# A context feed-forward network in plain fp32, and expert gates made on GpSimd, in a two-block transformer kernel

## The chip, the cores and the metric

One program runs on one core of a Trainium2 chip. The metric is the device time of one execution in microseconds. The engines are TensorE (PE in the rows; its weight loads are PEld), VectorE (DVE), ScalarE (ACT), GpSimd (POOL) and SyncE (SP), which issues most of the DMAs; each works through its own instruction list in order and waits on semaphores.

## The reference, cut to what matters

Two transformer blocks run one after the other, the second with two layers. The first block ends in an expert layer (`peer_ffn`): each of 512 tokens takes 8 heads x 16 experts out of 128 x 128 experts, and their gates weigh the experts' outputs. Layer 0 of the second block also carries a context stream of 256 tokens through mixers and a network of its own; layer 1 needs only the mixers' input of it.

```
    cv, ci = lax.top_k(cand.reshape(t, PEER_HEADS, PEER_TOPK * PEER_TOPK), PEER_TOPK)
    ...
    gates = jax.nn.softmax(cv, axis=-1).reshape(t, PEER_HEADS * PEER_TOPK)
...
def swiglu(h, w_gate, w_up, w_down):
    return (jax.nn.silu(h @ w_gate) * (h @ w_up)) @ w_down
...
        if need_ctx_out:
            xc = xc + g1c * yc
            hc = rms_norm(xc, norm_ffn[i]) * (1.0 + sc2c) + sh2c
            xc = xc + g2c * swiglu(hc, w_gate[i], w_up[i], w_down[i])
```

D_MODEL is 1024, D_FF 2816, and all arithmetic is float32.

## The kernel before, in words

**Slabs and units.** The weights come as slabs of 128 x 1024 floats (512 KB) into four landing slots `raw0` to `raw3`, issued by SP in the order of a list called `spine`. One slab is one unit of matmul work: eight 128 x 128 blocks. A normal unit is computed in three matmuls of type fp32r for each block: the slab is split into an upper part `whi` (ScalarE, L517) and a lower part `wlo` (VectorE or GpSimd, L525), the activations are split too (`hchi`/`hclo`, or `f10h` pairs inside the network), and the program adds whi x hi (L559), whi x lo (L561) and wlo x hi (L570): 24 fp32r matmuls a unit. The first two units after a norm are interleaved (`pair_tensor`, L589, L591, L596). A landing slot may be loaded again when its lower part has been made. A few small products stay plain fp32: one such matmul stands in the trace as two rows, an fp32r one as one row.

**The context network.** `cnet`, of class `Network`, has 66 units with 256 token columns: 44 for gate and up and 22 for down, in two halves of 11 hidden tiles. For each hidden tile ScalarE makes the silu (L3084 makes the upper half of the product), VectorE the product (L3072) and its lower half (L3076). The network's input comes from a norm applied in `Apply` (`c0ffn`: plain value `hct_plain`, then an upper and a lower part). Behind the network stand the norm of layer 1's context mixer (`c1mix`: sums L653 and L656) and that mixer's units and chains (called the c1 stage below); its last results are copied to `c_res` and stored by SP (L2369). Then come the 384-column units of the expert layer.

**Dense groups.** The gates of 384 tokens are spread into a dense 128 x 128 table per token. Work goes in 96 groups of four tokens. For a group k, VectorE compares an iota with the two halves of the expert number of every slot (L3403, one instruction for the two one-hots of four tokens, ring of four buffers `onehot`), ScalarE (48 groups, L3414, four instructions) or GpSimd (48, L3431) multiplies one of them by the gates, TensorE makes four plain fp32 128 x 128 matmuls (L3388, eight rows), ScalarE copies them to `stage` (L3422), and SP stores every fourth group in one DMA of 1 MB to `gate_dram`. A route stream must have finished a tile of 128 tokens before its 32 groups may begin. `gin0` and `gin1` are blocks of that table loaded back for the expert layer. The first expert rows are fetched by GpSimd with indirect DMAs (L3591) and dotted on VectorE (L3549).

**The order.** A planner written in Python (`Weave`) runs once when the program is built. It keeps a clock for each engine with costs from `Blank`, opens the units in spine order, puts a piece of the side streams (routing, dense groups, mixers' chains) between the ticks of a unit when its clocks say that the piece is ready, and writes each engine's instructions in a fixed order. On the chip only that order and the semaphores count. `split_ahead` puts splits up to two units ahead; `pump` releases side pieces. Where something must be complete (`drain`), what is left of the side streams is put in one block.

Of the kernel before, what the change touches and what calls it, by code (L numbers as in the profile page):

```python
# [367 lines left out]
class Unit:  # L368


    def __init__(self, kind, key, slab, n, groups, ring, lo="vector"):
        self.kind, self.key, self.slab, self.n, self.groups, self.ring, self.lo = kind, key, slab, n, groups, ring, lo
        self.each, self.need = False, None
# [49 lines left out]
def program(nc, io):  # L423
# [111 lines left out]
    def split_gpsimd(g, i):  # L535
        if spine[i].lo == "gpsimd":
            split_lower(g, i)

# [130 lines left out]
    class Apply:  # L669
# [3 lines left out]
        def __init__(self, name, nm, use, pairs, gain, shift=None, late=(), once=False, before=None, eps=EPS, tap=None,  # L673
                     root=True):
            self.name, self.nm, self.use, self.gain, self.shift, self.late = name, nm, use, gain, shift, late
            self.once, self.before, self.eps, self.tap, self.root = once, before, eps, tap, root
            self.pairs = [Pair(p.hi, p.lo, ("apply_a", name, "hi", c), self.lower_sig(c), p.plain) for c, p in enumerate(pairs)]
# [4 lines left out]
        def scalar(self, a):  # L682
# [31 lines left out]
        def vector(self, v):  # L714
# [11 lines left out]
            for c in range(3, KC) if self.once else [KC - 1]:  # L726
                self.lower_vector(v, c)

        def gpsimd(self, g):
            if self.once:  # L730
                for c in range(3):
# [2291 lines left out]
    class Network:  # L3023


        def __init__(self, l, v, n, pairs, places, ring, lo, free):
            self.l, self.v, self.n, self.free, nm = l, v, n, free, f"f{v}{l}"
            self.name = nm
            self.hid = [[sb(f"{nm}h{k}{y}", places[2 * k + y], [n], F32R)[:] for y in range(2)] for k in range(HALF)]
            self.sg = [sb(f"{nm}sg{i}", places[2 * HALF + i], [n])[:] for i in range(2)]  # L3030
            self.units = []
            for half in range(2):
                for k in range(HALF * half, HALF * half + HALF):
                    for kind, w in (("fgate", "w_gate2"), ("fup", "w_up2")):
                        u = Unit(kind, (self, k), io[w][l * 22 + k], n, [Group(pairs, (self, k))], ring, lo[half])
                        u.frees = (lambda out: [("ffn_a", out[0].name, "gate", out[1])]) if kind == "fgate" else \
                            (lambda out: [("ffn_v", out[0].name, "lo" if out[0].v else "up", out[1])])
                        self.units.append(u)
                for s in range(HALF):
                    groups = []  # L3040
                    for b in range(8 * s, 8 * s + 8):
# [3 lines left out]
                        groups[-1].pairs.append(Pair(*self.hid[k], ("ffn_a", nm, "hi", HALF * half + k), ("ffn_v", nm, "lo", HALF * half + k)))  # L3045
                        groups[-1].closes = k == HALF - 1
                    u = Unit("fdown", (self, half, s), io["w_down2"][(l * 2 + half) * HALF + s], n, groups, ring, lo[half])
                    u.frees = lambda out: [(x_flag(out[0].v), "down" if out[1] else "halfdown", out[0].l, out[2])]
                    self.units.append(u)

    def fgate_scalar(a, i, phase):
        f, k = spine[i].key
        a.wait_ge(*end(i))
        if k >= 2:
            a.wait_ge("ffn_v", f.name, "lo", k - 2)
# [6 lines left out]
    def product(f, k):  # L3062

        return held(("out", "fup", (f, k)))[:, 0:f.n] if f.v else f.sg[k % 2]
# [13 lines left out]
    def fup_scalar(a, i, phase):  # L3078
        f, k = spine[i].key
        if phase:  # L3080
# [1196 lines left out]
```

## Time and profile before

| | us |
|---|---|
| three runs, median | 3979.23 |
| lowest and highest | 3978.86 to 3980.32 |
| span of the profiled execution | 3975.2 |
| PE busy in it | 3796.6 (96%) |
| DVE busy | 2398.2 (60%) |
| ACT busy | 1638.3 (41%) |
| POOL busy | 775.2 (20%) |

The span is the time from the first to the last recorded instruction of one profiled execution; it is 4.0 us under the median of the runs, and what lies around it (the start and end of an execution) is in the runs' time and not in the span. Busy time of TensorE counts overlapping matmul records once.

### The profile page before, as it was taken

How to read it: one execution, taken by the hardware profiler on the slowest of the kernel's cores; microseconds unless marked ns; L12 is line 12 of the kernel's file. 1: busy time of each engine (PE TensorE's matmuls, PEld its weight loads, DVE VectorE, ACT ScalarE, POOL GpSimd, SP SyncE). 2: the span in 40 equal slices, each digit the busy share in tenths (PEclk: the TensorE clock that was granted, in tenths of full speed). 3: DMA queues.
4: the chain of work that ended last, by engine and by line, in shares of the span. 5: the costliest groups of instructions: out<-in, count | busy, mean ns of one | idle time of the engine just before them, and what ended most of it. 6: DMA issues, size and time to landing. Idle time of an engine off the chain costs nothing.

```text
span 3975.2 us, 57159 instructions
## 1 busy us (share of the span) xinstructions
PE 3796.6 (96%) x23057; PEld 3298.6 (83%) x23057; DVE 2398.2 (60%) x4113; ACT 1638.3 (41%) x2622; POOL 775.2 (20%) x622
## 2 busy tenths in 40 slices
PE   8999999989998889999999999998899999889998
PEld 5788776778898789999999999786678877667887
DVE  6455333546899977777777776557633345664333
ACT  4523342444456653333333333536522233563222
POOL 0112000244137443332223331201100010101000
PEclk9999999999999999999999999998999999999999
DMA  5211235533355488888888886311233342202332
GB/s 200 83 46 44 102 118 204 174 98 99 123 190 179 165 297 285 286 281 289 270 288 277 283 284 188 113 58 60 82 120 134 122 143 69 74 27 86 99 97 75
DMA packets 209190, 617.28 MB, mean 155 GB/s; under 512 B 18464, under 2 KB 68640, under 8 KB 205088
## 3 DMA queue, kind: packets, MB, share of 16 engines
q1 hardware_dynamic: 168352, 465.76, 35.8%
q0 software_dynamic: 40576, 147.87, 10.8%
q8 instruction: 183, 3.00, 0.3%
q14 instruction: 79, 0.65, 0.1%
HBM read 583.67 MB, written 29.88 MB: 154 GB/s over the span
## 4 chain that ended last, share of the span: by engine, by line
PE 81%; DVE 9%; ACT 5%; DMA 3%; issue 2%; POOL 0%; SPq 0%; DVEq 0%; ACTq 0%; POOLq 0%
PE ps L559 23%; PE ps L570 22%; PE ps L561 22%; PE ps L2468 1%; DVE hlo_plain L719 1%; PE ps L2495 1%; PE ps L842 1%; DMA raw<-w_in 1%; ACT whi L517 1%; DVE onehot L3403 1%; PE ps L2076 1%; PE ps L2486 1%; DMA gate_dram<-stage 1%; PE ps L1173 1%; PE ps L1164 1%
## 5 line engine op out<-in xcount | busy, mean ns | idle before, releaser
L525 DVE TENSOR_TENSOR wlo<-raw,whi 128x1024 fp32r<-128x1024 f32 x576 | 711.6, 1236 | 646.1 <-ACT whi L517 645.5
L559 PE MATMUL ps<-hhi,whi 128*128 128x512 f32 (+1 forms) x2824 | 1078.8, 382 | 18.2 <-ACT uact L3475 9.8
L561 PE MATMUL ps<-hlo,whi 128*128 128x512 f32 (+1 forms) x2824 | 1051.5, 372 | 0.1
L517 ACT ACTIVATE whi<-raw 128x1024 fp32r<-128x1024 f32 x660 | 695.2, 1055 | 629.8 <-PE ps L570 489.1
L570 PE MATMUL ps<-hhi,wlo 128*128 128x512 f32 (+1 forms) x2824 | 669.3, 375 | 0.0
L559 PEld LDWEIGHTS ps<-hhi,whi 128*128 128x128 f32 x2824 | 534.6, 189 | 120.7 <-issue 25.9
L561 PEld LDWEIGHTS ps<-hlo,whi 128*128 128x128 f32 x2824 | 535.0, 189 | 68.9 <-issue 4.1
L570 PEld LDWEIGHTS ps<-hhi,wlo 128*128 128x128 f32 x2824 | 512.6, 189 | 74.2 <-issue 7.2
L559 PE MATMUL ps<-ag_hi,whi 128*128 128x384 f32 x1024 | 342.7, 335 | 0.0
L561 PE MATMUL ps<-ag_lo,whi 128*128 128x384 f32 x1024 | 342.2, 334 | 0.0
L525 POOL TENSOR_TENSOR wlo<-raw,whi 128x1024 fp32r<-128x1024 f32 x85 | 206.6, 2441 | 162.3 <-ACT whi L517 162.2
L3591 POOL DMA_INDIRECT fetched<-peer_v_rows,rows x128 | 152.0, 1187 | 360.6 <-DVE xtok L3563 337.5
L3591 POOL DMA_INDIRECT fetched<-peer_u_rows,rows x128 | 151.5, 1183 | 340.9 <-DVE ract L3549 335.4
L3475 ACT ACTIVATE uact<-ps 128x384 f32<-128x384 f32 x128 | 62.9, 491 | 363.8 <-PE ps L570 363.8
L570 PE MATMUL ps<-ag_hi,wlo 128*128 128x384 f32 x1024 | 198.2, 334 | 0.0
L561 PEld LDWEIGHTS ps<-ag_lo,whi 128*128 128x128 f32 x1024 | 192.4, 188 | 0.0
L559 PEld LDWEIGHTS ps<-ag_hi,whi 128*128 128x128 f32 x1024 | 192.3, 188 | 0.0
L559 PE MATMUL ps<-hchi,whi 128*128 128x256 f32 x672 | 171.1, 290 | 16.2 <-ACT c_res L1935 4.6
L570 PEld LDWEIGHTS ps<-ag_hi,wlo 128*128 128x128 f32 x1024 | 179.3, 188 | 0.0
L3492 DVE TENSOR_TENSOR uact<-uact,gin 128x384 f32<-128x384 f32 x128 | 71.4, 558 | 163.6 <-ACT uact L3475 152.3
L644 POOL COPY nacc<-nsq 128x512 f32<-128x512 f32 x6 | 3.7, 609 | 851.2 <-ACT nsq L633 851.2
L561 PE MATMUL ps<-hclo,whi 128*128 128x256 f32 x672 | 167.2, 285 | 0.0
(653 smaller groups left out, 6233.1 us busy)
## 6 DMA issues: line engine op xcount, KB each, us to landing
raw<-w_in SPq DMA_DIRECT2D x151, 512.0 KB, 3.6
raw<-peer_u SPq DMA_DIRECT2D x128, 512.0 KB, 4.6
raw<-peer_v SPq DMA_DIRECT2D x128, 512.0 KB, 4.2
raw<-w_mod SPq DMA_DIRECT2D x96, 512.0 KB, 3.9
raw<-w_gate SPq DMA_DIRECT2D x66, 512.0 KB, 3.5
raw<-w_up SPq DMA_DIRECT2D x66, 512.0 KB, 3.5
raw<-w_down SPq DMA_DIRECT2D x66, 512.0 KB, 3.5
gate_dram<-stage SPq DMA_DIRECT2D x24, 1024.0 KB, 4.8
```

The costliest lines, as they stand in the source:

```text
L517: a.x.activation(whi[n % NW][:], raw[i % NRAW][:], ACT.Copy, bias=0.0, scale=1.0).then_inc(*a.gives("hi", i))
L525: e.x.tensor_tensor(wlo[n % NW][:], raw[i % NRAW][:], whi[n % NW][:].bitcast(F32), ALU.subtract).then_inc(*e.gives(*lo_sig(i)))
L559: t.x.matmul(o, w, p.hi, start=grp.opens and k == 0, stop=False)
L561: t.x.matmul(o, w, p.lo, start=False, stop=False)
L570: ins = t.x.matmul(o, lo[:, 128 * (starts[gi] + k):128 * (starts[gi] + k) + 128], p.hi, start=False, stop=grp.closes and k == len(grp.pair ...
L719: v.x.scalar_tensor_tensor(p.plain, self.nm.x[c], self.gain(c), self.nm.r[:], ALU.mult, ALU.mult).then_inc(*v.gives("apply_v", self.name, ...
L842: ins = t.x.matmul(bank[mod_at[l, r]][32 * j:32 * j + 32, :], svec[:, 2 * k:2 * k + 32], raw[i % NRAW][:, 512 * (j % 2):512 * (j % 2) + 51 ...
L1164: ins = t.x.matmul(b[r, h], heads(B2[:])[r, h, r], X[r, h], start=True, stop=True)
L1173: ins = t.x.matmul(b[r, h], Y[r, h], L[r, h], start=True, stop=True)
L3475: a.x.activation(uact[j % 2][:], held(("out", "peer_u", j))[:, 0:TD], ACT.Gelu_apprx_tanh, bias=0.0, scale=1.0).then_inc(*a.gives("peer_a" ...
L3492: v.x.tensor_tensor(t3, t3, gin[g % 2][:, :, jj, :], ALU.mult).then_inc(*v.gives("peer_v", "gated", j))
L3591: g.x.indirect_dma_start(fetched[i % NF][:], None, io["peer_v_rows" if i >= 128 else "peer_u_rows"], bass.IndirectOffsetOnAxis(ap=rows[:, ...
```

## The change

Three things are done. First, every unit of `cnet` is marked direct: TensorE multiplies the slab as it lies in its landing slot with the plain activations, eight plain fp32 matmuls instead of 24 of fp32r. Its split into `whi` and `wlo` is not made, the slot is free when the last matmul has ended, and neither the network's input nor its hidden tiles get a lower part (all eleven hidden tiles of a half stay whole in SBUF). Second, of every three dense groups one (k % 3 == 2) is made wholly by GpSimd: for each of its four tokens one instruction compares and multiplies by the gate (L3494 in the changed kernel) and one compares (L3496). Groups with k % 6 == 1 are still compared by VectorE and gated by GpSimd; ScalarE gates 48 groups as before. Third, the planner sees the new costs and lays everything out anew: all 96 dense groups now stand between units of the context network.

The core of the diff:

```diff
+    def split(i):
+        return spine[i].kind != "mod" and not spine[i].direct
...
     def load_sync(y, i):
         if i >= NRAW:
-            y.wait_ge(*(("mod_t", i - NRAW) if spine[i - NRAW].kind == "mod" else lo_sig(i - NRAW)))
+            before = spine[i - NRAW]
+            y.wait_ge(*(("mod_t", i - NRAW) if before.kind == "mod" else end(i - NRAW) if before.direct else lo_sig(i - NRAW)))
         y.x.dma_start(raw[i % NRAW][:], spine[i].slab).then_inc(*y.landing(f"raw{i % NRAW}", i))
...
+    def direct_tensor(t, i):
+        u, first, done = spine[i], 0, 0
+        w = raw[i % NRAW]
+        for gi, grp in enumerate(u.groups):
+            if grp.opens:
+                take(t, u.ring, ("out", u.kind, grp.out), *u.frees(grp.out))
+            o = held(("out", u.kind, grp.out))[:, 0:u.n]
+            t.wait_ge(f"raw{i % NRAW}", i)
+            for k, p in enumerate(grp.pairs):
+                t.wait_ge(*p.hi_sig)
+                ins = t.x.matmul(o, w[:, 128 * (first + k):128 * (first + k) + 128], p.plain, start=grp.opens and k == 0,
+                                 stop=grp.closes and k == len(grp.pairs) - 1)
+                done += 1
+                if k == len(grp.pairs) - 1:
+                    ins.then_inc(*t.gives("mm", i, gi))
+                if done in (2, 3, 4, 6, 7):
+                    yield
+            first += len(grp.pairs)
...
             for c, p in enumerate(self.pairs):
                 a.wait_ge("apply_v", self.name, "made", c)
+                if self.only:
+                    a.x.activation(p.plain, p.plain, ACT.Identity, bias=self.shift(c), scale=1.0).then_inc(
+                        *a.gives("apply_a", self.name, "moved", c))
+                    continue
...
+            for c in [] if self.only else range(3, KC) if self.once else [KC - 1]:
...
         if phase == 0:
             v.wait_ge(*end(i))
             v.wait_ge("ffn_a", f.name, "gate", k)
+            if f.whole and k >= HALF:
+                v.wait_ge(*last_of("fdown", (f, 0, (7 * HALF + k - HALF) // 8)))
             v.x.tensor_tensor(c, held(("out", "fup", (f, k)))[:, 0:f.n], f.sg[k % 2], ALU.mult).then_inc(*v.gives("ffn_v", f.name, "up", k))
-        else:
+        elif not f.whole:
             v.wait_ge("ffn_a", f.name, "hi", k)
             hi, lo = f.hid[k % HALF]
             v.x.tensor_tensor(lo, c, hi.bitcast(F32), ALU.subtract).then_inc(*v.gives("ffn_v", f.name, "lo", k))
...
-        freed[TABLE_BANK] = [("dense_v", NQ - 1), ("route_v", "looked", 3, 1)]
...
+        freed[TABLE_BANK] = [("dense_v", NQ - 2), ("route_v", "looked", 3, 1)]
...
-        return ("dense_g", k) if k % 2 else ("dense_a", k, "gated")
+        return ("dense_g", k, "made") if k % 3 == 2 else ("dense_g", k, "gated") if k % 6 == 1 else ("dense_a", k, "gated")
+    def compared(k):
+        return ("dense_g", k, "made") if k % 3 == 2 else ("dense_v", k)
...
-            if k < NQ:
+            if k < NQ and k % 3 != 2:
...
     def dense_gpsimd(g):
+        dense_free(g)
         for k in range(NQ + 3):
-            if 1 <= k <= NQ and k % 2 == 0:
+            if k < NQ and k % 3 == 2:
+                g.wait_ge("route_v", "tile", GT * k // 128)
+                if k >= 4:
+                    g.wait_ge("dense_t", k - 4)
+                for x in range(GT):
+                    n = GT * k + x
+                    g.x.tensor_scalar(ea[k % 4][:, x, :], cst[:, IOTA:IOTA + 128], iT[:, 0, n:n + 1], gT[:, n:n + 1], ALU.is_equal,
+                                      ALU.mult)
+                    ins = g.x.tensor_scalar(eb[k % 4][:, x, :], cst[:, IOTA:IOTA + 128], iT[:, 1, n:n + 1], None, ALU.is_equal)
+                ins.then_inc(*g.gives(*compared(k)))
+            if 1 <= k <= NQ and (k - 1) % 6 == 1:
...
-    cnet = Network(0, 1, TC, cffn.pairs, list(range(145, 152)) + list(range(168, 185)), "clate", ("vector", "gpsimd"), [])
+                 plain=True, late=[mod_ready(0)], before=("apply_v", "c0mix", "made", KC - 1))
+    cnet = Network(0, 1, TC, cffn.pairs, list(range(145, 152)) + list(range(168, 185)), "clate", ("vector", "gpsimd"), [], ("up", "down"))
```

**TensorE in the context network.** Line numbers of the changed kernel are higher: L559, L561 and L570 became L598, L600 and L609, L3388 became L3447, and L555 is the new direct matmul. Before, units of the second half read the upper part and the hidden halves (`f10h`), and now and then a dense group stands between them:

```order
L559 MATMUL ps<-f10h_253,whi_67 128x256
L561 MATMUL ps<-f10h_254,whi_67 128x256
L570 MATMUL ps<-f10h_261,wlo_70 128x256 [waits s_lo_g]
L570 MATMUL ps<-f10h_263,wlo_70 128x256
L570 MATMUL ps<-f10h_265,wlo_70 128x256
L570 MATMUL ps<-f10h_267,wlo_70 128x256
L3388 MATMUL ps<-onehot_204 128x128 [waits s_dense_v,s_dense_a]
L3388 MATMUL ps<-onehot_204 128x128 x3
```

Now, in the same network, plain matmuls on the slab alternate closely with dense groups:

```order
L3447 MATMUL ps<-onehot_205 128x128 [waits s_dense_v,s_dense_a]
L3447 MATMUL ps<-onehot_205 128x128 x3
L555 MATMUL ps<-hct_plain,raw_62 128x256 x3
L3447 MATMUL ps<-onehot_206 128x128 [waits s_dense_v,s_dense_a]
L3447 MATMUL ps<-onehot_206 128x128 x3
L555 MATMUL ps<-hct_plain,raw_62 128x256
L3447 MATMUL ps<-onehot_207 128x128 [waits s_dense_g,s_dense_a]
L3447 MATMUL ps<-onehot_207 128x128 x3
L555 MATMUL ps<-hct_plain,raw_63 128x256 [waits s_raw1,s_ffn_v]
```

The group in `onehot_207` waits for GpSimd alone (`s_dense_g`) beside its output bank. Of the 96 groups, 29 stood inside the network before, 4 behind its norm sum, 13 in the c1 stage and 50 after it; now 96 stand inside the network, the first after 84 of its 528 plain matmuls, and the last 104 of them have none.

**TensorE at the end of the c1 stage.** Before, the transposes of the last mixer results (L2347, L2392 in the changed kernel) were followed by dense groups only, up to the first expert unit:

```order
L2347 MATMUL ps<-cst,c_svT 128x128 [waits s_proj_a,s_store_v]
L2347 MATMUL ps<-cst,c_svT 128x128
L3388 MATMUL ps<-onehot_206 128x128 [waits s_dense_v,s_dense_a]
L3388 MATMUL ps<-onehot_206 128x128 x3
L3388 MATMUL ps<-onehot_207 128x128 [waits s_dense_v,s_dense_g,s_dense_a]
L3388 MATMUL ps<-onehot_207 128x128 x3
```

Now the expert unit follows at once:

```order
L2392 MATMUL ps<-cst,c_nvT 128x128 [waits s_store_v]
L2392 MATMUL ps<-cst,c_nvT 128x128
L2392 MATMUL ps<-cst,c_svT 128x128 [waits s_proj_a,s_store_v]
L2392 MATMUL ps<-cst,c_svT 128x128
L598 MATMUL ps<-hhi,whi_67 128x384 [waits s_hi]
L600 MATMUL ps<-hlo,whi_67 128x384
```

**VectorE at the first expert unit.** In the changed kernel the copies of the mixer's results, the first expert dot (L3619, which waits for the fetched rows) and the lower part of the third unit's slab follow each other:

```order
L530 TENSOR_TENSOR wlo_71<-raw_62,whi_68 128x1024 [waits s_hi,s_mm,s_raw0]
L2400 COPY c_res<-ps 128x2x128 [waits s_store_t] x2
L2400 COPY c_res<-ps 128x256 [waits s_store_t]
L3619 ISA fetched_218,ract<-fetched_218,xtok 128x1024 [waits s_fetched0,s_dense_t,s_tap_v]
L3619 ISA ract 128x1
L530 TENSOR_TENSOR wlo_69<-raw_63,whi_66 128x1024 [waits s_hi,s_mm,s_raw1]
```

Before, the dot and that lower part stood in the same order, behind the last one-hots of the dense groups. The load of `gin0` moved too: SP issues it in the c1 stage, between two loads of slabs, where before it came after the last dense store.

## Rows read from the trace of the kernel before

**Rows 1.** Windows of five stages: us, busy us (x instructions) of each engine, PEclk, DMA share, GB/s.

```profile
1057.00:1277.00 220.00, 218.57 (x1824) 217.58 (x1823) 210.32 (x489) 131.68 (x227) 102.26 (x57) 1.00 0.57 185
1277.00:1296.00 19.00, 8.63 (x36) 7.29 (x37) 15.02 (x23) 13.83 (x30) 9.97 (x8) 0.70 0.24 81
1296.00:1371.00 75.00, 63.58 (x488) 60.47 (x486) 67.23 (x82) 46.58 (x92) 36.79 (x20) 0.96 0.45 150
1371.00:1429.00 58.00, 51.09 (x401) 46.37 (x400) 55.56 (x51) 55.38 (x149) 25.99 (x25) 1.00 0.59 242
1429.00:1452.00 23.00, 13.20 (x77) 12.88 (x76) 4.27 (x7) 5.67 (x9) 6.49 (x6) 0.85 0.99 310
```

**Rows 2.** Timeline of PE, the network's last unit to the c1 stage: start, us, instruction, idle before.

```profile
1273.42 0.28 PE L561 MATMUL ps<-f10h,whi 128*128 128x256 f32 x1
...
1274.85 0.28 PE L561 MATMUL ps<-f10h,whi 128*128 128x256 f32 x1
1275.69 1.21 PE L570 MATMUL ps<-f10h,wlo 128*128 128x256 f32 x8 [0.56 <-POOL wlo L525]
...
1292.61 4.06 PE L3388 MATMUL ps<-onehot 128*128 128x128 f32 x16 [7.18 <-issue]
1296.32 0.56 PE L589 MATMUL ps<-hchi,whi 128*128 128x256 f32 x1
```

**Rows 3.** Timeline of PE, plain matmuls and what starts behind them.

```profile
956.43 1.56 PE L2468 MATMUL ps<-c_res,c_sq 64*128 64x256 f32 x6
957.92 0.51 PE L559 MATMUL ps<-hhi,whi 128*128 128x512 f32 x1
...
1130.95 1.06 PE L3388 MATMUL ps<-onehot 128*128 128x128 f32 x8
1131.76 0.36 PE L559 MATMUL ps<-f10h,whi 128*128 128x256 f32 x1
...
1333.78 1.03 PE L2041 MATMUL ps<-c_za,wa2c 128*128 128x256 f32 x4
1334.64 1.05 PE L3388 MATMUL ps<-onehot 128*128 128x128 f32 x8
```

**Rows 4.** Groups of DVE instructions by form, 1057 to 1277: busy us, mean ns, idle before.

```profile
L3403 DVE TENSOR_TENSOR onehot<-ps,iT 128x1024 f32<-128x1024 f32 x32 | 38.7, 1210 | 0.0
L525 DVE TENSOR_TENSOR wlo<-raw,whi 128x1024 fp32r<-128x1024 f32 x31 | 37.6, 1213 | 2.7 <-ACT whi L517 2.7
```

**Rows 5.** Timeline of PE, then of DVE, at the norm before the network.

```profile
1045.22 0.64 PE L570 MATMUL ps<-hchi,wlo 128*128 128x256 f32 x4
...
1056.36 0.56 PE L589 MATMUL ps<-hchi,whi 128*128 128x256 f32 x1 [3.35 <-ACT hchi L692]
...
1047.80 1.31 DVE L525 TENSOR_TENSOR wlo<-raw,whi 128x1024 fp32r<-128x1024 f32 x1 [1.50 <-ACT whi L517]
```

**Rows 6.** Waits of PE, 1277 to 1452: us in total, times, longest.

```profile
PE ps L559 <- ACT uact L3475: 9.8, 1, 9.8
```

**Rows 7.** Timeline of all engines at the first expert units, and landing of the c_res store.

```profile
1429.64 1.05 POOL L3591 DMA_INDIRECT fetched<-peer_u_rows,rows  x1 [1.93 <-PE ps L3388]
...
1436.43 1.23 DVE L3549 CUSTOM_DVE_ANT_0 fetched<-fetched,xtok 128x1024 f32<-128x1024 f32 x1 [9.84 <-DMA fetched<-peer_u_rows,rows]
...
1451.65 0.69 PE L559 MATMUL ps<-hhi,whi 128*128 128x384 f32 x1 [9.80 <-ACT uact L3475]
...
DMA to landing us min/median/max: 5.7/5.7/5.7
```

**Rows 8.** Groups of POOL instructions by form, whole span: busy us, mean ns, idle before.

```profile
L644 POOL COPY cnacc<-cnsq 128x256 f32<-128x256 f32 x3 | 1.3, 422 | 192.8 <-ACT cnsq L633 192.8
L644 POOL COPY nacc<-nsq 128x512 f32<-128x512 f32 x6 | 3.7, 609 | 851.2 <-ACT nsq L633 851.2
L3431 POOL TENSOR_TENSOR onehot<-onehot,gT 128x512 f32<-128x512 f32 x48 | 52.9, 1103 | 116.6 <-DVE onehot L3403 116.6
L647 POOL TENSOR_TENSOR cnacc<-cnacc,cnsq 128x256 f32<-128x256 f32 x15 | 13.4, 896 | 15.8 <-ACT cnsq L633 15.5
```

More of the change, by code:

```diff
@@ L372, in __init__ @@
         self.kind, self.key, self.slab, self.n, self.groups, self.ring, self.lo = kind, key, slab, n, groups, ring, lo
-        self.each, self.need = False, None
+        self.each, self.need, self.direct = False, None, False
 class Group:
@@ L537, in split_gpsimd, with direct_pair_tensor @@
             split_lower(g, i)
+    def direct_tensor(t, i):
[16 more added lines that the diff above has]
+            first += len(grp.pairs)
+    def direct_pair_tensor(t, i0):
+        two = (i0, i0 + 1)
+        outs = [take(t, spine[i].ring, ("out", spine[i].kind, spine[i].groups[0].out), *spine[i].frees(spine[i].groups[0].out))
+                [:, 0:spine[i].n] for i in two]
+        for k, p in enumerate(spine[i0].groups[0].pairs):
+            for i, o in zip(two, outs):
+                t.wait_ge(f"raw{i % NRAW}", i)
+                t.wait_ge(*p.hi_sig)
+                ins = t.x.matmul(o, raw[i % NRAW][:, 128 * k:128 * k + 128], p.plain, start=k == 0, stop=k == KC - 1)
+                if k == KC - 1:
+                    ins.then_inc(*t.gives("mm", i, 0))
+            yield
     def unit_tensor(t, i):
@@ L730, in gpsimd @@
             if self.once:
-                for c in range(3):
+                for c in range(0 if self.only else 3):
                     p = self.pairs[c]
@@ L3023, in program, with __init__ @@
     class Network:
-        def __init__(self, l, v, n, pairs, places, ring, lo, free):
+        def __init__(self, l, v, n, pairs, places, ring, lo, free, direct=()):
             self.l, self.v, self.n, self.free, nm = l, v, n, free, f"f{v}{l}"
-            self.name = nm
+            self.name, self.direct = nm, direct
+            self.whole = [sb(f"{nm}w{k}", places[2 * k], [n])[:] for k in range(HALF)] if "down" in direct else None
             self.hid = [[sb(f"{nm}h{k}{y}", places[2 * k + y], [n], F32R)[:] for y in range(2)] for k in range(HALF)]
             self.sg = [sb(f"{nm}sg{i}", places[2 * HALF + i], [n])[:] for i in range(2)]
+            self.taken = "lo" if v and not self.whole else "up"
             self.units = []
@@ L3079, in fup_scalar @@
         f, k = spine[i].key
-        if phase:
+        if phase and not f.whole:
             a.wait_ge("ffn_v", f.name, "up", k)
@@ L3409, in dense_scalar @@
         for k in range(NQ + 3):
-            if 1 <= k <= NQ and k % 2:
+            if 1 <= k <= NQ and gated(k - 1)[0] == "dense_a":
                 a.wait_ge("dense_v", k - 1)
@@ L3678, in program @@
         place_of[u.kind, u.key] = i
-        if u.kind != "mod":
+        if split(i):
             nth[i] = len(nth)
@@ L3759, in perform @@
             if e.name == "tensor":
-                e.going["unit"] = unit_tensor(e, what) if kind == "open" else pair_tensor(e, what, piece[2])
+                if spine[what].direct:
+                    e.going["unit"] = direct_tensor(e, what) if kind == "open" else direct_pair_tensor(e, what)
+                else:
+                    e.going["unit"] = unit_tensor(e, what) if kind == "open" else pair_tensor(e, what, piece[2])
         elif kind == "tick":
@@ L3795, in split_next @@
         at_unit["split"] += 1
-        if spine[i].kind != "mod":
+        if split(i):
             plan.put("split", i)
@@ L3854, in unit @@
                 plan.pump()
+        if u.direct:
+            raw_done(i)
         evacuate(i, *([1] if u.each else []))
@@ L3891, in pair @@
             elif n == 11:
+                if spine[i].direct:
+                    raw_done(i)
+                    raw_done(i + 1)
                 evacuate(i + 1)
```

26 lines of the change are left out of this document (16 added, 10 removed).

## The prediction

> **What bounds the kernel now.** I read the windows by stage first. In the context network TensorE is busy 218.57 of 220 us at full clock, and VectorE 210.32 of 220: TensorE sets the time, with VectorE close behind. Then come three places where it doesn't: the norm behind the network (8.63 busy of 19), the c1 stage (63.58 of 75) and the block of dense groups behind it (51.09 of 58) [rows 1]. That block has 401 matmul rows, 50 groups of eight, in 58 us, 1.16 us a group, while VectorE is busy 55.56 us with one-hots of 1.21 us [rows 1, 4]: VectorE sets the pace there. At the expert layer's start TensorE waits once more, 9.8 us, for the first activations [rows 6]. So the change can gain where TensorE idles and must pay where it is full, and the sum is made on TensorE's list.
>
> **What the direct units cost.** Twelve steps of fp32r matmuls with 256 columns take 1274.85 - 1273.42 = 1.43 us, 0.12 each [rows 2]; a block needs three, 0.36, a unit 2.88. A plain fp32 matmul of the same size stands once as two in a row: 1333.78 to 1334.64, 0.86, so 0.43 each [rows 3]. The bounds: four with 128 columns take 1131.76 - 1130.95 = 0.81, so 0.405 for 256 columns; three with 64 rows of weights take 957.92 - 956.43 = 1.49, 0.50 each with the change into and out of them [rows 3]. I take 0.43, same shape and same engine state. 66 units x 8 = 528 blocks, each 0.43 - 0.36 = 0.07 dearer: **+37.0 us**, from +24 (0.405) to +74 (0.50).
>
> The Trainium skill speaks against the change too ("FP8 and Floating Point Precision", TensorE Precision Notes): true fp32 takes four passes through the array. By passes alone, an estimate from that page, three passes of fp32r would turn into four and 528 x 256 columns at 2.4 GHz would add 56 us; the rows, where an fp32r step is 0.120 and a plain one 0.43, give +37, and I go by the rows.
>
> **What it gives back on TensorE's list.**
> - The block of dense groups: its 50 groups move between the network's units. At the 0.9 us that a group occupies (0.81, and the next matmul starts 0.08 late) [rows 3], they are 45 of the 58 us; the other **13** vanish.
> - The norm behind the network. From the last matmul of the last unit (1275.69 + 1.21, its tail off, 1276.8) to the c1 stage's first (1296.32) are 19.5 us [rows 2], 3.6 of them four dense groups. 7.18 us of the wait end at 1292.61 with no releaser shown. The same norm before the network, without dense work in the way, goes from 1045.22 + 0.5 to 1056.36, 10.7 us, with two lower parts (one of 1.31, after a wait of 1.50 for ScalarE) inside its chain [rows 5]. Without one-hots ahead of it on VectorE I take about 8 for the coming one: 15.9 - 8, **-7.7** (0 if the cause of the 7.18 stays; -9 at most).
> - The c1 stage idles 75 - 63.58 = 11.4 us, with VectorE busy 67.23 of 75 [rows 1]. 13 groups leave; VectorE's chains then wait for fewer one-hots, but TensorE's waits lose their filling. **-3** (0 to -11.4).
> - The start of the network: its first two slabs are no longer split, so VectorE's 1.31 and the wait of 1.50 for ScalarE's upper part [rows 5] leave the norm's chain: **-2** (0 to -3).
> - Small waits in the network (220 - 218.57): **-1.2**.
> - The wait of 9.8 at the expert layer. The mixer's results must be stored before the expert rows are fetched (the landing of that store took 5.7), the fetch took 1436.43 - 1429.64 = 6.8 [rows 7], and in the new order on VectorE the first dot stands ahead of the third expert unit's lower part, with the wait for the store now in its way: the dot begins some 15 us after the last copy X (2.5 to the store, 5.7, 6.8), the lower part is made 2.4 later (1.23 and 1.2) at X + 17.4, and TensorE wants it at about X + 11, two and a half units later (an estimate of 4.3 us each: 24 matmuls of 384 columns at 0.12 for 256). So about 6.4 us of wait stand where 9.8 did: **-3.4** (0 to -9.8). Who is queued behind that dot on VectorE: this lower part, then the gates' product that feeds the next activations.
>
> Sum: 13 + 7.7 + 3 + 2 + 1.2 + 3.4 = 30.3.
>
> **What the hand-over costs.** VectorE loses its 31 lower parts in the network and makes 64 one-hots there, where 32 stood [rows 4]: 210.3 - 37.6 + 32 x 1.21 = 211 us in some 316, so it is hidden on average. But a route tile, whose work is VectorE's, must end before its 32 groups, and where the planner's clock and the chip's differ, a group's first matmul waits a little. No row of before shows such dense alternation, so I put **+3** on late hand-overs (0 to +8).
>
> GpSimd's new instruction, 128x128, one input and two scalars, isn't in the trace. A copy takes 422 ns at 256 and 609 at 512 columns [rows 8], by that line 0.33 at 128: eight make 2.6 us. The upper bound is the line through the two-input forms, 896 at 256 and 1103 at 512 [rows 8]: 0.79 at 128, 6.3 a group; the lower one is the copies' fixed part, 0.235, 1.9 a group. Behind the third route tile 68 groups share some 200 plain matmuls, (200 x 0.43 + 68 x 0.9) / 68 = 2.2 us a group, 2.0 where they are densest. There a GpSimd group and the gating behind it (1.10) [rows 8] must fit between the end of the group that frees the buffer and three places later, 3 x 2.0 - 0.9 = 5.1 us. 2.6 + 1.1 + 0.3 for semaphores = 4.0 fits: **0**. Above about 0.46 each (3.7 a group) TensorE waits.
>
> The Trainium skill ("GPSIMD Engine Reference", section 3.1 Elementwise) has the body of such an instruction bound by its ports, at best 769 ns for 512 elements, so some 0.19 us for 128; an estimate from it is 1.5 us a group. That leaves the 0 of the sum and speaks against rival D.
>
> Slab loads: a slot is now free at the end of a unit and not at its split, so a load starts three units ahead, 10 us, and the DMA share in the network is 0.57 [rows 1]: hidden. The load of `gin0` (1.5 MB) now competes with the slabs of the c1 stage, DMA share 0.45 [rows 1], in 75 us: **+1** (0 to +6, if SP's queue holds a slab up).
>
> Sum: 37.0 - 30.3 + 3 + 1 = 10.7, say +10. On the profiled execution's own time, 3975.2 + 10 = 3985 span, and the median is 4.0 above its span: **3989 us**.
>
> **The rivals.**
> - *A, the forecast*: the plain passes cost more than the idle time gives back: 3987.2 to 3997. What speaks for it: TensorE is full at 218.57 of 220, the price is a row's. Chance 0.43.
> - *B, it cancels out*: hand-overs are free (-3 against A) and c1's idle shrinks by 5 or 6 in place of 3, the norm's by 9: +37 - 13 - 9 - 6 - 2 - 1.2 - 4 = +2, from -7 to +7, 3981. For it: the c1 stage's VectorE is 90% busy, and one-hots leave it. Against: its waits are chains that TensorE's matmuls themselves are part of. Chance 0.32.
> - *C, faster*: the one mechanism is VectorE's relief behind the network. If one-hots ahead of the chains are what makes c1 idle, all 11.4 go, and the store of the results then lies so early that the 9.8 go too: 37 - 13 - 7.7 - 11.4 - 2 - 1.2 - 9.8 = -8, 3971. The idle time left behind the network's end (norm, c1, expert start) is 8 + 8.4 + 6.4 = 23 in A and 8 here; the sign turns at 23 - 10.7 = 12. A plain matmul at 0.405 (-13) leads there as well. Chance 0.12.
> - *D, GpSimd is the bound*: at 0.6 us each a group takes 4.8, and each of some 12 late turns waits 1.1, +13: about 4001; at 0.79 it is some +31. A plain matmul at 0.47 in the network (+21) gives 4009. For it: two-input forms are that dear; against: copies aren't. Chance 0.13.
>
> **How the numbers follow.** The time is A's. One case in ten may lie under 3972 (half of C) and one above 4008 (a third of D): range 3972 to 4008; A's own is 3987 to 3997. 0.2%, 8 us, is about what a measurement of this kernel can tell from no change: slower by more is A and D, 0.43 + 0.13, with A's lower edge just above that line, so 0.55; within it B and the edges of C, 0.34; faster 0.11.
>
> **What the changed kernel's profile would show.** The network lasts from about 1054 to about 1372 (66 x 3.44 + 96 x 0.9 + 3 = 316 us), with all 96 groups inside; plain matmuls start 0.43 apart; eight GpSimd instructions sum to 2.6 us a group; TensorE's waits for one-hots sum to 3 us; the norm behind it takes 8 us, the c1 stage about 60 with 8 or 9 idle; no block of dense groups; the first expert unit begins near 1440; before the third stand 6 us of wait. The prediction is wrong if plain matmuls start under 0.41 or over 0.45 apart, if waits for `onehot` pass 8 us, or if the idle time behind the network isn't 23 us within 6.

## The result and the profile after

The changed kernel takes 4005.22 us (median of 4 runs, 3999.72 to 4006.42), the kernel before 3979.05 (4 runs): 1.006 of it, interval 1.0048 to 1.0072. That is 26 us or 0.6% slower, clear of the 0.2% bound. A second series beside other kernels gave 4000.87 against 3980.56, 1.0053 (1.0036 to 1.0070). The forecast was 3989; the range, 3972 to 4008, holds the result.

The windows of the changed kernel's profile (us, busy us of each engine with its instructions, PEclk, DMA share, GB/s), cut at its own stages: the network, the norm behind it, the c1 stage, the first expert units.

```profile
1052.80:1396.70 343.90, 322.60 (x1841) 290.81 (x1842) 208.30 (x498) 144.22 (x347) 205.48 (x280) 0.99 0.53 173
1396.70:1402.00 5.30, 1.79 (x8) 0.91 (x6) 1.65 (x4) 3.08 (x6) 0.45 (x1) 0.93 0.70 265
1402.00:1459.30 57.30, 51.49 (x372) 49.47 (x373) 32.23 (x52) 32.78 (x55) 31.52 (x17) 0.92 0.48 141
1459.30:1480.00 20.70, 11.51 (x67) 11.19 (x66) 3.08 (x6) 3.16 (x4) 5.94 (x6) 0.83 0.85 296
```

Against [rows 1]: the network grew from 220.4 us (1056.36 to 1276.8, [rows 2, 5]) to 343.9, of which TensorE idles 21.3 where it idled 1.4; the norm fell from 19.5 to 5.3; the c1 stage and the block behind it, 132.8 together, became 57.3. VectorE, 67.23 busy of 75 before, is busy 32.23 of 57.3. The span is 4004.6 in an execution whose time was 4006.42.

The waits of TensorE, 1040 to 1480 (us in total, times, longest), four of its rows:

```profile
PE ps L3447 <- issue: 19.4, 8, 2.7
PE ps L609 <- DVE wlo L530: 9.2, 1, 9.2
PE ps L598 <- ACT c_nvT L1980: 3.5, 1, 3.5
PE ps L3447 <- ACT onehot L3473: 1.9, 1, 1.9
```

The first row names no engine; the timelines of PE and then of POOL show who it was.

```profile
1319.21 1.05 PE L3447 MATMUL ps<-onehot 128*128 128x128 f32 x8
...
1322.72 1.05 PE L3447 MATMUL ps<-onehot 128*128 128x128 f32 x8
1323.61 0.60 PE L555 MATMUL ps<-hct_plain,raw 128*128 128x256 f32 x2
1326.95 1.13 PE L3447 MATMUL ps<-onehot 128*128 128x128 f32 x8 [2.74 <-issue]
...
1340.46 2.05 PE L3447 MATMUL ps<-onehot 128*128 128x128 f32 x8 [2.74 <-issue]
...
1320.37 0.80 POOL L3494 TENSOR_SCALAR onehot<-cst,iT,gT 128x128 f32<-128x128 f32 x1 [0.22 <-PE ps L3447]
1321.15 0.60 POOL L3496 TENSOR_SCALAR onehot<-cst,iT 128x128 f32<-128x128 f32 x1
...
1325.24 0.60 POOL L3496 TENSOR_SCALAR onehot<-cst,iT 128x128 f32<-128x128 f32 x1
1325.81 1.04 POOL L3501 TENSOR_TENSOR onehot<-onehot,gT 128x512 f32<-128x512 f32 x1
```

GpSimd's eight instructions last from 1320.37 to 1325.81, the gating of the group before them ends at 1326.85, and TensorE, which stands at that group, goes on at 1326.95. The group GpSimd made itself comes later and isn't waited for. All eight waits of the first row, and the one of 1.9 us that is put down to ScalarE (ACT), end 0.1 us behind such a gating; six of the nine are 2.7 us long, the other three 1.5, 1.6 and 1.9. Behind the second stall shown, the last of the nine, the eight rows take 2.05 us; behind each of the others they take 1.13, and without a stall 1.05. Three windows with the same columns as above, ahead of the first stall shown, behind the second, and the whole stretch of low clock around the latter:

```profile
1322.00:1324.00 2.00, 2.00 (x15) 1.70 (x13) 1.04 (x2) 0.68 (x3) 2.00 (x4) 1.00 0.48 197
1340.40:1343.50 3.10, 3.04 (x12) 2.89 (x13) 0.00 (x0) 0.70 (x2) 0.88 (x2) 0.50 0.00 0
1339.80:1346.60 6.80, 6.14 (x23) 5.63 (x24) 0.00 (x0) 2.74 (x7) 4.55 (x7) 0.50 0.41 137
```

The granted clock is 1.00 (2.4 GHz) in the first and 0.50 (1.2 GHz) in the other two. Between the two stalls shown (1327.0 to 1339.8) it is 1.00: behind the first it did not fall.

### The profile page after: what moved, and what is told of

It reads as the page before. It is cut to its first block, busy times and chain, and to the rows that moved or that the text cites. A ratio compares the mean times of both kernels' runs of the same rounds, so it can differ in the third digit from the quotient of the medians.

```text
span 4004.6 us, 55994 instructions
## 1 busy us (share of the span) xinstructions
PE 3831.3 (96%) x22529; PEld 3307.7 (83%) x22529; DVE 2290.1 (57%) x4021; ACT 1567.6 (39%) x2529; POOL 838.3 (21%) x810
## 4 chain that ended last, share of the span: by engine, by line
PE 85%; DVE 6%; ACT 4%; DMA 2%; issue 2%; POOL 0%; SPq 0%; DVEq 0%; ACTq 0%; POOLq 0%
PE ps L598 22%; PE ps L609 21%; PE ps L600 21%; PE ps L555 5%; PE ps L3447 2%; PE ps L2513 1%; PE ps L2540 1%; PE ps L887 1%; DMA raw<-w_in 1%; DVE hlo_plain L764 1%; ACT whi L522 1%; PE ps L2531 1%; PE ps L2121 1%; PE ps L1218 1%; PE ps L1209 1%
## 5 line engine op out<-in xcount | busy, mean ns | idle before, releaser
L598 PE MATMUL ps<-hhi,whi 128*128 128x512 f32 (+1 forms) x2824 | 1076.2, 381 | 6.1 <-DVE xres L3049 2.9
L600 PE MATMUL ps<-hlo,whi 128*128 128x512 f32 (+1 forms) x2824 | 1049.7, 372 | 0.1
L530 DVE TENSOR_TENSOR wlo<-raw,whi 128x1024 fp32r<-128x1024 f32 x543 | 671.3, 1237 | 635.5 <-ACT whi L522 627.3
L522 ACT ACTIVATE whi<-raw 128x1024 fp32r<-128x1024 f32 x594 | 625.7, 1054 | 598.5 <-PE ps L609 453.8
L609 PE MATMUL ps<-hhi,wlo 128*128 128x512 f32 (+1 forms) x2824 | 670.3, 376 | 9.2 <-DVE wlo L530 9.2
L598 PEld LDWEIGHTS ps<-hhi,whi 128*128 128x128 f32 x2824 | 533.4, 189 | 108.3 <-issue 23.1
L600 PEld LDWEIGHTS ps<-hlo,whi 128*128 128x128 f32 x2824 | 533.4, 189 | 69.0 <-issue 4.1
L609 PEld LDWEIGHTS ps<-hhi,wlo 128*128 128x128 f32 x2824 | 513.0, 189 | 83.8 <-DVE wlo L530 9.5
L600 PE MATMUL ps<-ag_lo,whi 128*128 128x384 f32 x1024 | 342.0, 334 | 0.0
L598 PE MATMUL ps<-ag_hi,whi 128*128 128x384 f32 x1024 | 342.0, 334 | 0.0
L609 PE MATMUL ps<-ag_hi,wlo 128*128 128x384 f32 x1024 | 198.2, 334 | 0.0
L598 PEld LDWEIGHTS ps<-ag_hi,whi 128*128 128x128 f32 x1024 | 192.2, 188 | 0.0
L600 PEld LDWEIGHTS ps<-ag_lo,whi 128*128 128x128 f32 x1024 | 192.1, 188 | 0.0
L609 PEld LDWEIGHTS ps<-ag_hi,wlo 128*128 128x128 f32 x1024 | 179.3, 188 | 0.0
L3619 DVE CUSTOM_DVE_ANT_0 fetched<-fetched,xtok 128x1024 f32<-128x1024 f32 x128 | 156.0, 1218 | 17.4 <-DMA fetched<-peer_u_rows,rows 17.4
L3633 DVE SCALAR_TENSOR_TENSOR xtok<-fetched,ract,xtok 128x1024 f32<-128x1024 f32 x127 | 162.4, 1279 | 0.0
L555 PE MATMUL ps<-hct_plain,raw 128*128 128x256 f32 x672 | 160.5, 382 | 0.0
```

Of the source, the lines that this page charges most:

```text
L522: a.x.activation(whi[n % NW][:], raw[i % NRAW][:], ACT.Copy, bias=0.0, scale=1.0).then_inc(*a.gives("hi", i))
L530: e.x.tensor_tensor(wlo[n % NW][:], raw[i % NRAW][:], whi[n % NW][:].bitcast(F32), ALU.subtract).then_inc(*e.gives(*lo_sig(i)))
L555: ins = t.x.matmul(o, w[:, 128 * (first + k):128 * (first + k) + 128], p.plain, start=grp.opens and k == 0, stop=grp.closes and k == len(g ...
L598: t.x.matmul(o, w, p.hi, start=grp.opens and k == 0, stop=False)
L600: t.x.matmul(o, w, p.lo, start=False, stop=False)
L609: ins = t.x.matmul(o, lo[:, 128 * (starts[gi] + k):128 * (starts[gi] + k) + 128], p.hi, start=False, stop=grp.closes and k == len(grp.pair ...
```

## The experiments

The cause that the trace points to was **theory 1**: GpSimd's one-hots are dear, and TensorE waits for what is queued behind them. **Theory 2**, the rival: the plain units, or their alternation with dense groups, cost more than their rows say, or VectorE's relief works some other way. All ran in three series of four kernels, each series beside the kernel before (medians 3979.79, 3980.88 and 3980.56). The network's start differs by up to 6 us between profiled executions of kernels whose instructions up to there are nearly the same (1056.36 in the kernel before, 1050.65 in e9), so times between kernels are read from the medians, and profiles within a stretch.

**e1, the direct units alone.**

```diff
-        return ("dense_g", k, "made") if k % 3 == 2 else ("dense_g", k, "gated") if k % 6 == 1 else ("dense_a", k, "gated")
+        return ("dense_g", k, "gated") if k % 2 else ("dense_a", k, "gated")
...
-            if k < NQ and k % 3 != 2:
+            if k < NQ:
```

> The direct units alone; every one-hot is VectorE's again and ScalarE and GpSimd gate 48 groups each, as before. Theory 1 (GpSimd's one-hots are late: 5.6 us a group; 21 us of TensorE's idle time in the network and some 4 us of a lower clock behind the stalls): both go, 4005 - 24 = about 3981, VectorE at 208 + 39 = 247 us in 320, all waits of TensorE for one-hots under 4 us in sum. Theory 2 (the alternation of plain matmuls with dense groups, or the plain units, cost more than their rows say): the time stays at 3998 or more with the waits gone.

Measured: 3976.58 us (3972.22 to 3981.92), 0.9991 of before (0.9982 to 1.0001). Its windows, network, norm and c1 stage:

```profile
1052.00:1369.30 317.30, 317.30 (x1841) 288.96 (x1842) 246.17 (x530) 147.11 (x349) 60.19 (x56) 0.99 0.57 188
1369.30:1374.60 5.30, 1.73 (x7) 0.89 (x6) 1.71 (x5) 3.14 (x6) 0.46 (x1) 0.85 0.73 262
1374.60:1430.80 56.20, 50.87 (x372) 49.02 (x373) 29.96 (x52) 32.69 (x55) 32.74 (x17) 0.92 0.48 144
```

All 96 groups stand in the network here too, and TensorE idles not at all; VectorE's 246.17 lie beside 317.30. The network is 26.6 us shorter than with GpSimd's one-hots: 21.3 of idle time and 322.60 - 317.30 = 5.3 in which TensorE counts as busy. Only a part of the 5.3 is the lower clock: in e14, the changed kernel once more, the clock stayed at 1.00 behind every stall, and TensorE was busy 319.69 of 340.97 us. So about 2.9 us belong to the one fall of the clock, and some 2.4 are left for the nine interruptions themselves; the loss by GpSimd's lateness is 24 to 27 us. The planner put the groups elsewhere than in the changed kernel, but about as close: the last 68 of them come one every 3.1 plain matmuls, against 3.0. Theory 1 stands, and the plain units cost what their rows say.

**e2, GpSimd's dense groups alone.**

```diff
-                 plain=True, late=[mod_ready(0)], before=("apply_v", "c0mix", "made", KC - 1))
+                 late=[mod_ready(0)], before=("apply_v", "c0mix", "made", KC - 1))
-    cnet = Network(..., [], ("up", "down"))
+    cnet = Network(..., [])
```

> GpSimd's dense groups alone; the network is computed from split slabs in fp32r as before. Theory 1: six groups take GpSimd 2 x 5.6 + 1.04 = 12.2 us, 2.04 a group, where VectorE set 1.16; some 46 groups in the block behind the c1 stage become 46 x 0.88 = 40 us slower: about 4010 to 4020. Theory 2: GpSimd's price does no harm, the block is relieved of a third of VectorE's one-hots: 3965 to 3979.

Measured: 4048.73 us, 1.0175 (1.0158 to 1.0192), worse than expected. The last window is the block of dense groups behind the c1 stage:

```profile
1054.00:1303.00 249.00, 232.74 (x1865) 230.12 (x1865) 221.27 (x500) 142.25 (x251) 168.61 (x141) 0.96 0.53 172
...
1383.00:1500.00 117.00, 68.61 (x423) 65.08 (x422) 42.91 (x44) 58.52 (x152) 100.97 (x145) 0.82 0.33 133
```

423 rows, some 53 groups, in 117 us: 2.2 a group, not 2.04, GpSimd busy 100.97. The network itself (1053.99 to 1300.97; the window above ends 2 us behind it) grew from 220 to 247 us, of which the four more groups in it explain 3.6. TensorE's waits there sum to 16 us, the longest in total for lower parts on GpSimd (8.2 us), whose list also holds the one-hots, and its clock is 0.96 where [rows 1] have 1.00. That was not in the expectation. The norm behind the network, from 1300.97 to the mixer's first matmul at 1306.54, takes 5.6 us, with the units split as before and no dense group in it.

**e3, the gating ahead of the one-hots.**

```diff
     def dense_gpsimd(g):
         dense_free(g)
         for k in range(NQ + 3):
+            if 1 <= k <= NQ and (k - 1) % 6 == 1:
+                ...
             if k < NQ and k % 3 == 2:
                 ...
-            if 1 <= k <= NQ and (k - 1) % 6 == 1:
-                ...
```

> The changed kernel, but GpSimd gates the group k - 1 before it makes the group k, not behind it. Theory 1, as a latency: the gating (1.04) no longer waits behind 5.6 us of one-hots, and these have four places instead of three; stalls of 2.74 us fall under 1, about 3988 (3984 to 3993). As a throughput (GpSimd full with 12.2 us in six groups against TensorE's 12 to 13): stalls stay nearly as long at another place, 4000 or more. Theory 2: 4005 within 3.

Measured: 3988.39 us (3984.02 to 3991.42), 1.0021 (1.0011 to 1.0030). The row of its waits that is left for one-hots:

```profile
PE ps L3447 <- POOL onehot L3500: 8.1, 7, 1.3
```

19.4 us in stalls of up to 2.7 became 8.1 in stalls of at most 1.3, now for GpSimd's own groups. TensorE's order is the changed kernel's but for two of the 96 groups, which moved by at most two plain matmuls, so the order of two steps on GpSimd alone was worth some 13 to 15 us (by the ratios to the kernel before, against both series of the changed one): the stall was a latency in the first place, with little slack behind it.

**e5, GpSimd's true price in the planner.**

```diff
-    tensor_scalar = memset = light
+    memset = light
+    def tensor_scalar(self, out, *a, **k):
+        if self.name == "gpsimd":
+            self.spent += 0.70 / 128 * width(out)
+            return self
+        return self.light(out)
```

> The changed kernel with the planner's cost of a 128x128 GpSimd tensor_scalar set to the measured mean 0.70 us in place of 0.22. The last group stands behind 494 of 528 plain matmuls instead of 424, 68 groups on 268 plain matmuls behind the third tile: 2.6 us a group, 3 x 2.6 - 0.9 = 6.9 us for the 5.6 + 1.04 + 0.3. Theory 1: stalls nearly gone, 3981 to 3987. Theory 2: 4005 within 4.

Measured: 3977.39 us (3972.63 to 3985.50), 0.9995 (0.9986 to 1.0005). Its network:

```profile
1052.40:1371.00 318.60, 318.59 (x1841) 289.93 (x1842) 207.52 (x498) 143.82 (x347) 202.90 (x280) 0.99 0.56 187
```

The instructions are the same, their places differ (66 of the 96 groups stand further back), and no idle time is left. The time is below the 3981 to 3987 expected. It is as fast as e1 and no faster: VectorE's 39 us less buy nothing.

**e6, the expert dots later (on e1).**

```diff
-    plan.start("experts", streams["experts"])
+    plan.start("experts", streams["experts"], delay=8.0)
```

> The direct units alone, and the stream of expert dots starts 8 us later in the planner's time, so that VectorE's first dot (which waits for the fetched rows) stands behind the lower parts of the third and fourth expert units. Theory 1 (the 9.6 us of TensorE's wait at the expert layer are the third unit's lower part queued behind that dot): the wait falls under 2, 3976.6 - 8 = about 3968. Theory 2 (the lower part is only the name; the rows fetched by GpSimd or the load of the gates end the wait anyway): another wait of 7 to 10 us takes its place, 3974 to 3978.

Measured: 3967.23 us (3963.09 to 3971.52), 0.9963 (0.9951 to 0.9976). VectorE of the changed kernel, then of e6, after the last copies:

```profile
1459.58 0.42 DVE L2400 COPY c_res<-ps 128x256 f32<-128x256 f32 x1 [0.20 <-PE ps L2392]
1477.43 1.23 DVE L3619 CUSTOM_DVE_ANT_0 fetched<-fetched,xtok 128x1024 f32<-128x1024 f32 x1 [17.42 <-DMA fetched<-peer_u_rows,rows]
1478.58 0.08 DVE L3619 DVE_READ_ACCUMULATOR2_ANT ract<- 128x1 f32 x1
1478.58 1.22 DVE L530 TENSOR_TENSOR wlo<-raw,whi 128x1024 fp32r<-128x1024 f32 x1
```

```profile
1430.39 0.42 DVE L2400 COPY c_res<-ps 128x256 f32<-128x256 f32 x1 [0.20 <-PE ps L2392]
1430.73 1.22 DVE L530 TENSOR_TENSOR wlo<-raw,whi 128x1024 fp32r<-128x1024 f32 x1
...
1436.14 1.22 DVE L530 TENSOR_TENSOR wlo<-raw,whi 128x1024 fp32r<-128x1024 f32 x1 [0.49 <-ACT whi L522]
...
1447.30 1.23 DVE L3619 CUSTOM_DVE_ANT_0 fetched<-fetched,xtok 128x1024 f32<-128x1024 f32 x1 [7.49 <-DMA fetched<-peer_u_rows,rows]
```

The dot waits nearly as long, 16.5 us behind the last copy's end (17.4 in the changed kernel), but the lower part that TensorE needs is made ahead of it, and the wait of 9.6 us is gone.

**e7 and e8, only the down units direct, and only the gate and up units.**

```diff
-    cnet = Network(..., [], ("up", "down"))
+    cnet = Network(..., [], ("down",))
```

> Only the 22 down units direct, the 44 gate and up units split as before; dense groups made by VectorE as before. TensorE's work grows by 176 x 0.07 = 12.3 us instead of 37. 54 groups stand inside the network, 42 outside (of before 29 and 67, of all units direct 96 and 0). Theory 1 (the gain of the direct units comes from placing dense groups where VectorE is relieved, in proportion to the groups moved): 25 of 67 groups bring about 0.37 of the 39.7 us of idle time that all direct units gave back, 15: 3979.5 + 12.3 - 15 = 3977. Theory 2 (the norm and the start give back the most, whatever moves): 3979.5 + 12.3 - 25 = 3967.

> Only the 44 gate and up units direct; work +24.6 us. 52 groups inside, 44 outside. Theory 1: 23 of 67 moved, 14 us back: 3979.5 + 24.6 - 14 = 3990. Theory 2: 3979.5 + 24.6 - 25 = 3979. By the plain matmul's price (0.43 against 0.36) this one is some 12 us above the one with the down units alone under either.

Measured: e7 3967.00 us (3964.87 to 3972.60), 0.9966 (0.9953 to 0.9978); e8 3977.47 (3972.39 to 3982.34), 0.9993 (0.9983 to 1.0002). The 10.5 us between them are the price of 22 units more (about 12 expected). But the gain is not in proportion to the dense groups moved: e7 gives back 13.9 + 12.3 = 26 us with 54 groups inside. In e7's timeline of PE the norm behind the network:

```profile
1309.18 0.59 PE L692 MATMUL ps<-cnacc,ones 128*128 128x256 f32 x2
...
1310.37 0.70 PE L695 MATMUL ps<-cnsq,ones 128*128 128x256 f32 x2 [0.16 <-ACT cnsq L672]
1314.48 0.35 PE L628 MATMUL ps<-hchi,whi 128*128 128x256 f32 x1 [3.41 <-ACT hchi L737]
```

5.3 us, as with all units direct (and 5.6 in e2, whose units are all split), and here no dense group stands in it. In the kernel before the mixer's first matmul was queued behind four dense groups. Two rows of its timeline, of ACT and of POOL, show when the mixer's input was there and what the third of those groups waited for:

```profile
1285.54 1.31 ACT L692 ACTIVATE hchi<-hct_plain,mod 128x256 fp32r<-128x256 f32 x3 [0.61 <-DVE hct_plain L719]
...
1291.29 1.22 POOL L3431 TENSOR_TENSOR onehot<-onehot,gT 128x512 f32<-128x512 f32 x1
```

The mixer's first input was there at about 1286; TensorE stood until 1292.61 at a group whose gating had to queue on GpSimd behind the norm's own work, and reached the mixer at 1296.32. This is read from the trace; no run moved these four groups alone.

**e9, the kernel before with the expert dots later** (the edit of e6).

> The kernel before with the expert dots 8 us later in the planner's time. There gin0 is loaded behind the last dense store, and landed just before the wait of 9.8 us ended. Theory 1: that wait is the gates' load, so it stays at 7 to 10 us and the time within 2 us of before. Theory 2: it is the lower part behind the first dot, as in the changed kernel: 8 us faster, 3971.

Measured: 3978.95 us (3974.20 to 3984.00), 0.9997 (0.9988 to 1.0007). VectorE:

```profile
1445.95 0.56 DVE L3492 TENSOR_TENSOR uact<-uact,gin 128x384 f32<-128x384 f32 x1 [16.27 <-DMA gin<-gate_dram]
```

The same wait of TensorE, 8.3 us here, had another owner before the change: the gates, stored and loaded only after the last dense group. In the kernel before itself VectorE idles 11.3 us for that load.

**e10 and e11, the whole change repaired** (the edits of e3, e5 and e6 together), with all units direct, and with the down units alone.

> The whole change with three repairs: the planner's cost for GpSimd's instruction 0.70 us, the gating ahead of the one-hots, and the expert dots 8 us later. Theory 1 (lateness of GpSimd and the lower part behind the first dot are all that the change loses): the gain of the planner's cost (3977.4) and of the later dot (-9) add up: 3968, no better than the direct units alone with the later dot (3967.2), since VectorE has room for all one-hots. Rival (GpSimd's one-hots are worth something once they are on time): under 3963.

> Only the down units direct, GpSimd makes every third dense group, with the same three repairs. 65 groups stand inside the network, 31 outside, where GpSimd needs 2 x 5.6 + 1.04 = 12.2 us for six and VectorE alone 7.3. Theory 1: 31 groups cost about 31 x 0.85 = 26 us more than with VectorE alone (where TensorE waits for them one by one), less the 11 moved inside: 3967 + 15 to 25 = 3982 to 3992. Rival (relief of VectorE is what counts in this form too): 3960 or less.

Measured: e10 3971.52 us (3966.04 to 3973.52), 0.9972 (0.9961 to 0.9984); e11 3994.07 (3992.86 to 4009.10), 1.0042 (1.0026 to 1.0058), 27 us above e7, at the far end of what was expected and only in part by that mechanism. GpSimd's one-hots gain nothing where VectorE has room. In e11 they cost at two places. Behind the network's norm TensorE waits 11.3 us for them, and 104.8 us hold 31 groups where e7's 102.3 hold 42. Inside the network it waits 11.2 us for lower parts that GpSimd makes too, which e7 does not, and that network lasts 285.9 us against 256.0, where 11 more groups explain 10: the larger part of the loss, and the expectation had nothing of it.

**e12, every sixth group by GpSimd.**

```diff
-        return ("dense_g", k, "made") if k % 3 == 2 else ("dense_g", k, "gated") if k % 6 == 1 else ("dense_a", k, "gated")
+        return ("dense_g", k, "made") if k % 6 == 2 else ("dense_g", k, "gated") if k % 2 == 1 else ("dense_a", k, "gated")
```

> The changed kernel with every sixth dense group (k % 6 == 2) made by GpSimd in place of every third, and the odd groups gated by it as before. In six groups GpSimd has 5.6 + 3 x 1.04 = 8.7 us to do instead of 12.2. Theory 1 as a throughput: no stalls, 3978 (as the direct units alone). As a latency (group 6m + 1 is gated behind the 5.6 us of group 6m + 2, three places of 2.0 us to do both in): the same stall once in six groups, 2.7 x 8 = 20 us, 3995 to 4005.

Measured: 4004.95 us (4001.70 to 4008.95), 1.0059 (1.0043 to 1.0076). TensorE's wait:

```profile
PE ps L3447 <- issue: 18.9, 9, 2.7
```

Half of GpSimd's one-hots, and the same loss; the planner put nearly all groups elsewhere, but about as close as before. With e3 this settles it: not the sum of GpSimd's work counts (8.7 of some 13 us) but the 5.6 us in one piece ahead of a gating that is due.

**e14, the changed kernel once more.**

> The changed kernel once more, beside the others on one chip: 4005 within 3, TensorE's waits for one-hots again about 2.7 us once in six groups.

Measured: 4000.87 us (3999.05 to 4006.30), 1 us outside what was expected, and again 19.4 us of waits in 8 stalls and one of 1.9. The network takes 341.0 us here and 343.9 in the first profile, with the same instructions in the same order on TensorE: the difference is the clock behind the last stall.

## Why the prediction was right in sign and 16 us short

Term by term, as the prediction put them:

- *The direct units, +37.0.* Right. In the changed kernel plain matmuls run in long rows:

```profile
1061.46 25.20 PE L555 MATMUL ps<-hct_plain,raw 128*128 128x256 f32 x116
1086.50 0.27 PE L3225 MATMUL ps<-cst,chosen 128*128 128x128 f32 x1
```

  58 matmuls in 25.04 us, 0.432 each: 528 x (0.432 - 0.36) = 38. The Trainium skill's estimate by passes ("FP8 and Floating Point Precision", TensorE Precision Notes), +56, was too high. Without stalls the network is 317.3 us long (e1), where 316 was forecast.
- *The dense block and the c1 stage, -13 and -3.* 132.8 us less 63 groups of 0.9 were 76.1 and are 57.3: -18.8. The sum was 2.8 short.
- *The norm, -7.7.* 15.9 became 5.3: -10.6. The cause lay in the order, as the trace shows it: a dense group ahead of the mixer on TensorE, its gating behind the norm on GpSimd. The direct units are not needed for it: e2, which has none, shows nearly the same short norm (5.6).
- *The start, -2.* From the last matmul's end at 1045.9 (its tail off, as in the prediction) to 1052.80 are 6.9 us, before 10.6 [rows 5]: -3.7.
- *The expert layer's wait, -3.4.* 9.2 instead of 9.8: -0.6. The mechanism was the one forecast (e6), its size was off: the dot began 17.4 us behind the last copy's end, not 15. The store left at 1460.04, and the first fetch was issued only at 1468.18, 8.1 us later, where the sum had 5.7.
- *The load of gin0, +1.* Nothing of it can be seen.
- *Late hand-overs, +3, and GpSimd's price, 0.* **This is the step that failed.** The room was put at 5.1 us for one-hots, gating and 0.3; the instruction was put at 0.33 by the line through the copies, 2.6 a group. In the network of the changed kernel the groups on POOL have (busy us, mean ns):

```profile
L3494 POOL TENSOR_SCALAR onehot<-cst,iT,gT 128x128 f32<-128x128 f32 x128 | 106.6, 832 | 104.1 <-PE ps L3447 59.0 <-DVE gT L3409 41.0 <-DVE cand L3313 3.9
L3496 POOL TENSOR_SCALAR onehot<-cst,iT 128x128 f32<-128x128 f32 x128 | 78.3, 611 | 0.0
```

  0.80 us for the two operations and 0.60 for the one in most of them, 5.6 us a group. With 1.04 and 0.3 that is 6.9 against 5.1, late by 1.8. The room was mis-sized too: at the stall shown the group that frees the buffer ends at 1320.26 (1319.21 + 1.05) and TensorE wants the gated one at 1324.21 (1326.95 - 2.74), 4.0 us later and not 5.1. So 6.9 against 4.0 makes the 2.7 us, to 0.2; at the forecast price of 2.6 a group, 4.0 in all, there would still have been next to no stall. It is rival D, whose price at 0.6 us was forecast as +13, twelve turns of 1.1; nine turns cost 21.3 us of idle time, and 26.6 in all in this execution (2.9 of it by the clock, 2.4 around the stalls).

The estimate from the Trainium skill's "GPSIMD Engine Reference" (section 3.1, Elementwise) was 0.19 us an instruction; here a 128x128 one takes three to four times that. The trace does not agree with it, and the estimate by it would have led to the same 0 in the sum.

The sum with measured terms: 38 - 18.8 - 10.6 - 3.7 - 1.4 - 0.6 = +2.9 without GpSimd's lateness (e1's medians say -3.2, interval -7 to +0.4; its profiled execution was one of its slowest, with a span 4.6 above that of before), and 26.6 more with it, +29.5, which is the difference of the two spans, 4004.6 - 3975.2 = 29.4. The medians differ by 26: the prediction's "4.0 around the span" was mostly scatter between executions, since the changed kernel's profiled one has 1.8.

So the sign was right by luck. The mechanism of the forecast, plain passes that cost more than the idle time gives back, was to make +10; without GpSimd's lateness the terms sum to +2.9, and e1 is no slower than the kernel before (0.9991). What made the kernel slower is the step that the sum had at 0, and the range holds the result by rival D, to which the prediction gave 0.13. Of its three signs of being wrong one was met: the waits for `onehot` were 21.3 us, not under 8; plain matmuls started 0.432 apart, within 0.41 to 0.45, and the idle time behind the network was 20.3, within 23 and 6.

Rival C's mechanism was at work in part: the norm, the c1 stage's idle time and the expert layer's wait are 5.3 + 5.8 + 9.2 = 20.3 us here, and about 11 in e6 (the direct units alone with the later dot), under the 12 at which the sign was to turn; e6 is faster by 0.37%.

What stays open: why the networks of e2 and e11 are longer than their groups explain was read from the profile only (lower parts on GpSimd beside its one-hots, and the clock) and not tried by itself. Why the clock fell behind one stall of 2.74 us and not behind others of the same length, no run tells. Nor was a kernel tried that has GpSimd's one-hots on time and VectorE scarce in the network, so their worth in such a place is unknown. A form with few wide instructions in place of the eight was not tried.

## What to carry to other kernels

Price an offloaded instruction in its own form and width before moving many small ones, not by a line through other forms: eight of 0.6 to 0.8 us for 128 columns made a block of 5.6 us where one VectorE instruction of 1.21 had stood. What hurts then is what is queued behind that block on its engine; putting the short urgent step first (e3) or correcting the one number in the planner (e5) gave back some 13 to 15 and some 23 to 26 us without any change in the work. Plain fp32 in place of three fp32r passes costs 20% of TensorE's time here (0.432 against 0.36) and is repaid only by idle time elsewhere, so take it for no more units than it needs: 22 units gave 3967.0 where 66 gave 3976.6 (e7 and e1), or 3967.2 with the dots later (e6). And a wait at a stage's border can change its owner without changing its length (e9 against e6).

## What the runs showed of the hardware

GpSimd's tensor_scalar on 128x128 floats took 0.60 us with one per-partition scalar and 0.80 with two, where a two-input one on 128x512 took 1.04. TensorE's granted clock was 0.50 from 1339.8 to 1346.6, behind one of nine stalls in the changed kernel, and eight rows that take 1.05 us took 2.05; behind the others, four of them as long to 0.01 us, they took 1.13, and in e14, the same kernel, they did so behind all nine. In e12 it fell behind three of eight. Behind the norm and a wait of 3.41 us the mixer's matmuls started 0.21 us apart for 6 us in the changed kernel; in e7, behind a wait of the same length, the first four started 0.12 apart, and only after them, from 1315.4 to 1318.8, was the clock 0.50 and the distance 0.21. Why it falls at one such place and not at another, no run tells.
